# Recurrence of a hybrid HGRN2 / RWKV-7 layer: inverse levels laid over the whole array, reordered score, y and token products, loads in two parts

## The chip, the cores and the metric

One NeuronCore of a Trainium2 chip. The metric is the device time of one execution in microseconds (us). All data is fp32. [...]

## The reference

One step of a hybrid layer for 2048 tokens of a new stream ("prompt") and 8 running streams of 16 tokens ("sample"). RMSNorm and modulation; an input projection; two groups of heads on the same input; an output projection; a two-level mixture of experts; a final RMSNorm. The change is in the two groups of heads:

```
HGRN2, 4 heads of 128:     S_t = diag(f_t) S_{t-1} + k_t v_t^T,  o_t = S_t^T q_t   (chunks of 64 tokens)
RWKV-7, 8 heads of 64:     S_t = S_{t-1}(diag(w_t) - kk_t^T (a_t*kk_t)) + v_t^T k_t,  y_t = S_t r_t
```

with a normalisation and a gate on o and y, and the last states as outputs.

## The kernel before, in words

The program has four stages, each with its own block of engine programs and semaphores: `project`, `recur`, `merge`, `experts`. `project` leaves in DRAM the scaled factors of both groups (`rk`: five rows A0, A1, B0, B1, V for RWKV; `hk`: six level factors, B, KD, Q, K for HGRN2) and token rows (`tm`). Only `recur` is changed.

`recur` goes over 17 frames of 128 tokens (two chunks of 64 on the two halves of the partitions); frame 16, `TAIL`, holds the sample. In pass i of the main loop the front of frame f = i is interleaved with the back of frame b = i - 1. The order of each engine's instructions is written out by hand; semaphores tie the engines.

**Front of a frame.** `turn` transposes V, B0 and B1 into tokens (ScalarE copies them, `keep_tok`). `products` forms B·A for B0 and B1, 16 products of 64x64 by 128 columns each, and VectorE masks them (`mask_products`) into LB (the strictly causal matrix to be inverted, and its y part) and MK. RWKV's delta rule needs for every head and chunk the inverse of a 64x64 unit triangular matrix. It is built by doubling, levels 1 to 5 (in `TAIL` to 3): `begin_xt` and `turn_x0` set up level 0, and at each level `make_y` forms Y = L·X, VectorE masks it (`mask_y`), `turn_x` transposes X, ScalarE copies the transpose (`keep_xt`), `make_x` multiplies XT and Y and adds into X's bank, and ScalarE copies X (`keep_x`). The last level is `make_xt`, kept by `keep_xtf`. Each of these steps is 16 matmuls of 64x64 by 64, for 8 heads and 2 chunks; input rows `chunk(c)` always give output partitions `chunk(c)`. Beside the levels `score` forms HGRN2's seven score matrices, two a time in one bank (the last alone), VectorE merges them under level masks (`mask_score`), `turn_kd` transposes KD, and `from_tokens` starts g and y from the values.

**Back of a frame.** Chunk by chunk: `h_update`, `h_inter`, `h_intra` (HGRN2); `from_state`, `from_values`, `solve` (with the inverse), `to_state`, `y_from_state`, `y_out` (RWKV). Then VectorE and ScalarE normalise and gate o and y into `mix`, which SyncE stores.

PSUM: P_X, P_Y, P_XT, P_S serve the inverse, the products, the scores and the HGRN2 update in turn; P_ST (half used) the RWKV state, P_O o, P_EO g and y.

**Loads.** SyncE issues all. `load_front(f)` brings rk and hk of a frame with 8 DMAs on one semaphore; frame i + 2 is requested when KD of frame i is transposed (`kd_made`). `load_back` brings A, B and the token rows. At the start all loads of front 0 and the two `even` masks stand ahead of the first wait.

The sequence of TensorE around the levels, before:

```
                for lv in range(2, levels(f)):
                    make_y(f, lv)
                    turn_x(f, lv - 1)
                    score(f, lv - 1)
                    if lv < levels(f) - 1:
                        make_x(f, lv)
                    else:
                        make_xt(f)
                turn_kd(f)
                from_tokens(f)
```

Of the kernel before, what the change touches and what calls it, by code (L numbers as in the profile page):

```python
# [22 lines left out]
CH = 64  # L23
# [863 lines left out]
def recur(nc, t, bonus, ends):  # L887

    names = []
    with ExitStack() as ctx:  # L890
# [28 lines left out]
        Y = sb("Y", [128, 8, CH])  # L919
        Y1, Y3, Y5 = [sb(f"Y{n}", [128, 8, CH]) for n in (1, 3, 5)]  # L920
# [20 lines left out]
        sumd = sb("sumd", [128, 2, 4, RW_N])  # L941
# [8 lines left out]
        P_X, P_Y, P_XT, P_S, P_ST, P_O = [ctx.enter_context(nc.psum_tensor(f"re_P{b}", [128, 512], F32)) for b in range(6)]  # L950
# [3 lines left out]
        TAIL = PT  # L954

# [38 lines left out]

        block = ctx.enter_context(nc.Block())

        @block.sync
        def _(eng):
            eng.dma_start(const[:, :, :].rearrange("p a b -> p (a b)"), t["const"]).then_inc(ev("const_in"), 16)
            rk3 = t["rk"].rearrange("(c s p) w -> p c s w", p=128, s=N_RK)  # L1000
            hk3 = t["hk"].rearrange("(c s p) w -> p c s w", p=128, s=N_HK)

            def load_front(f):

                k, p = 128 * f, f % 2
                for c in range(4):
                    eng.dma_start(rkf[p][:, c, :, :], rk3[:, c, :, k:k + 128]).then_inc(ev(f"front_in{p}"), 16)
                for c in range(4):
                    if f < TAIL:
                        eng.dma_start(hkf[p][:, c, :, :], hk3[:, c, :, k:k + 128]).then_inc(ev(f"front_in{p}"), 16)  # L1010
                    else:
                        for s0, s1 in ((0, levels(f)), (N_LEVELS, N_HK)):
                            eng.dma_start(hkf[p][:, c, s0:s1, :], hk3[:, c, s0:s1, k:k + 128]).then_inc(ev(f"front_in{p}"), 16)
# [9 lines left out]
            load_front(0)  # L1023
            eng.dma_start(even[:, :, :].rearrange("p a b -> p (a b)"), t["even"]).then_inc(ev("const_in"), 16)
            eng.dma_start(even_row[:, :], t["even_row"]).then_inc(ev("const_in"), 16)
# [3 lines left out]
            load_front(1)  # L1029
            load_back(1)  # L1030
            eng.dma_start(Sd[:, :, :, :], t["state_hgrn"][0].rearrange("s h k v -> k s h v")).then_inc(ev("state_in"), 16)
# [30 lines left out]
        def _(eng):  # L1062
            eng.wait_ge(ev("const_in"), 48)


            def h_update(b):
# [4 lines left out]
                eng.wait_ge(ev("xtf_kept"), 2 * b + 2)  # L1071
                for h in range(4):
                    o = slice(128 * h, 128 * h + 128)
                    for c in range(2):
                        ins = eng.matmul((P_S, P_XT)[c][:, o], kdT[p][chunk(c), o], tmb[p][chunk(c), 0, o], start=(h == 0), stop=(h == 3), skip_group_check=True)
# [47 lines left out]
            def from_values(b, c):  # L1123

                p = b % 2
                if b or c:
                    eng.wait_ge(ev("st_kept"), 2 * b + c)
                for h in range(8):
                    eng.matmul(out_st(half(h), h), tok[p][chunk(c), 2, 64 * h:64 * h + 64], tok[p][chunk(c), 0, 64 * h:64 * h + 64],
                               start=(h < 2), stop=False, skip_group_check=True)  # L1130

            def solve(b, c):

                p = b % 2
                eng.wait_ge(ev("g_kept"), 2 * b + c + 1)
                for h in range(8):
                    ins = eng.matmul(out_g(chunk(c), h), XTF[p][chunk(c), h, :], G[chunk(c), 64 * h:64 * h + 64],
                                     start=False, stop=(h == 7), skip_group_check=True)
# [28 lines left out]

            def products(f, kind, banks):

                p = f % 2  # L1170
                for h in range(8):
                    o = 128 * (h // 2)
                    for c in range(2):
                        ins = eng.matmul(banks[h % 2][chunk(c), o:o + 128].rearrange("p (a b) -> p a b", a=2), rkf[p][half(h), h // 2, kind, chunk(c)],
                                         rkf[p][half(h), h // 2, RK_A0:RK_A1 + 1, chunk(c)], start=(h < 2), stop=(h >= 6), skip_group_check=True)
# [3 lines left out]
            def turn_x0(f):  # L1179

                eng.wait_ge(ev("xt0_made"), 2 * f + 2)
                for h in range(8):
                    for c in range(2):
                        ins = eng.matmul(P_S[chunk(c), 64 * h:64 * h + 64], XT0[chunk(c), h, :], ident[chunk(c), chunk(c)], start=(h == 0), stop=(h == 7), skip_group_check=True)
                ins.then_inc(ev("x0_made"), 1)

            def make_y(f, lv):

                if lv == 1:
                    eng.wait_ge(ev("x0_kept"), f + 1)  # L1190
                    eng.wait_ge(ev("product_kept"), 4 * f + 4)
                for g in range(2):
                    if lv > 1:
                        eng.wait_ge(ev("x_kept"), before(f, 8) + 2 * (lv - 2) + g + 1)
                    for h in range(4 * g, 4 * g + 4):
                        for c in range(2):
                            ins = eng.matmul(P_Y[chunk(c), 64 * h:64 * h + 64], LB[f % 2][chunk(c), h, 0, :], X[chunk(c), h, :],  # L1197
                                             start=(h == 0), stop=(h % 4 == 3), skip_group_check=True)
                ins.then_inc(ev("y_made"), 1)

            def turn_x(f, lv):

                for h in range(8):
                    for c in range(2):
                        ins = eng.matmul(P_XT[chunk(c), 64 * h:64 * h + 64], X[chunk(c), h, :], ident[chunk(c), chunk(c)], start=(h == 0), stop=(h == 7), skip_group_check=True)  # L1205
                ins.then_inc(ev("xt_made"), 1)

            def make_x(f, lv):

                for g in range(2):  # L1210
# [1345 lines left out]
```

## Time and profile before

| what | value |
|---|---|
| median of 3 runs | 3289.81 us (3288.94 to 3295.39) |
| the profiled execution | 3291.22 us, its span 3289.4 us |
| granted clock over the span | 0.963 |
| `project` (0 to 1105.6) | TensorE busy 1023.2 of 1105.6 us |
| `recur` (1105.6 to 1848) | TensorE busy 643.4 of 742.4 us, VectorE 403.0, ScalarE 213.3 |
| `merge` and `experts` (1848 to the end) | TensorE busy 1349.6 of 1441.4 us |

Times in the rows are us from the start of the span. In the profile PE is TensorE's matmuls, PEld its weight loads, DVE VectorE, ACT ScalarE, SPq the issuing of DMAs by SyncE. Every fp32 matmul is recorded as two, so 16 matmuls stand as x32. Matmul ends are modelled; starts are better to go by.

### The profile page before, as it was taken

The numbers are of one execution on the slowest core, as the hardware profiler recorded it, in microseconds if no ns is written. First come the engines' busy times: TensorE is split into PE (matmuls) and PEld (weight loads), VectorE is DVE, ScalarE is ACT, GpSimd is POOL, SyncE is SP. The second block draws the span as 40 slices with busy tenths as digits, with TensorE's granted clock in tenths as the row PEclk, the third lists the DMA queues.
The fourth block names the chain that finished last, engine by engine and source line by source line (L and its number), as shares of the span: only waits on it lengthen the run. The fifth ranks groups of instructions, "written<-read, shape, count | busy, mean of one in ns | idle before, by whom it ended". The sixth has DMA issues, their size and how long they took to land. (4 is left out here: it accounts for less than half of the span.)

```text
span 3289.4 us, 68115 instructions
## 1 busy us (share of the span) xinstructions
PE 3016.1 (92%) x28667; PEld 1817.9 (55%) x28668; DVE 1407.8 (43%) x3436; ACT 977.0 (30%) x1872; POOL 161.9 (5%) x248
## 2 busy tenths in 40 slices
PE   5998999999999399999998599958999999999998
PEld 2432455454545288888888355535555555555543
DVE  2255466655557355555556244452111122111217
ACT  2456334333434223332333112111222222222215
POOL 0000000000000000000000000000000000000004
PEclk8999999999999799999999699978999999999998
DMA  7631123232322755555552643355786577667658
GB/s 269 214 116 55 49 97 129 104 126 91 122 83 101 224 151 150 150 152 159 158 158 74 182 172 115 115 169 168 290 333 240 185 279 283 239 251 281 236 201 332
DMA packets 373225, 575.73 MB, mean 175 GB/s; under 512 B 31230, under 2 KB 230966, under 8 KB 369944
## 3 DMA queue, kind: packets, MB, share of 16 engines
q1 hardware_dynamic: 340296, 474.06, 42.7%
q0 software_dynamic: 18080, 72.10, 6.3%
q10 hardware_dynamic: 14640, 26.49, 2.7%
q8 instruction: 167, 2.74, 0.3%
q14 instruction: 42, 0.34, 0.0%
HBM read 427.04 MB, written 145.54 MB: 174 GB/s over the span
## 5 line engine op out<-in xcount | busy, mean ns | idle before, releaser
L451 PE MATMUL pj_P<-pj_hT,pj_wc 128*128 128x448 f32 (+2 forms) x1600 | 590.4, 516 | 0.9 <-ACT pj_stage L579 0.9
L2429 PE MATMUL moe_PG<-wgu,moe_xT 128*64 128x256 f32 x5248 | 582.1, 380 | 0.7 <-ACT moe_xT L2327 0.7
L2429 PEld LDWEIGHTS moe_PG<-wgu,moe_xT 128*64 128x64 f32 x5248 | 377.3, 137 | 226.3 <-issue 47.4
L451 PEld LDWEIGHTS pj_P<-pj_hT,pj_wc 128*128 128x128 f32 x1600 | 294.1, 189 | 256.5 <-issue 239.4
L2436 PE MATMUL moe_PTY<-wd,moe_hT 128*64 128x512 f32 x1312 | 317.7, 603 | 0.0
L2330 ACT ACT_TABLE_LOAD x82 | 105.2, 1283 | 484.2 <-issue 484.1
L1916 PE MATMUL merge_PO<-merge_w,merge_mT 128*128 128x512 f32 x544 | 244.4, 608 | 3.5 <-DMA merge_w<-in_w_out 3.5
L1916 PEld LDWEIGHTS merge_PO<-merge_w,merge_mT 128*128 128x128 f32 x544 | 104.6, 195 | 130.2 <-issue 130.2
L2289 DVE TENSOR_TENSOR moe_sg<-moe_sg,moe_PG 128x128 f32<-128x128 f32 x164 | 46.3, 282 | 283.9 <-ACT moe_sg L2330 283.9
L2293 DVE COPY moe_hT<-moe_PH 128x128 f32<-128x128 f32 x164 | 47.8, 291 | 279.9 <-PE moe_PH L2421 279.9
L2436 PEld LDWEIGHTS moe_PTY<-wd,moe_hT 128*64 128x64 f32 x1312 | 81.9, 136 | 120.2 <-issue 86.8
L2296 DVE COPY moe_y<-moe_PTY 128x512 f32<-128x512 f32 x82 | 56.7, 692 | 208.3 <-PE moe_PTY L2436 208.3
L1197 PE MATMUL re_P<-re_X,re_LB 64*64 64x64 f32 x2656 | 97.4, 220 | 28.4 <-ACT re_X L1448 23.0
L372 PE MATMUL pj_P<-pj_wt,pj_hT 128*128 128x512 f32 x272 | 122.5, 604 | 0.0
L482 PE MATMUL pj_P<-pj_wt,pj_hT 128*128 128x512 f32 x272 | 121.3, 599 | 0.0
L1197 PEld LDWEIGHTS re_P<-re_X,re_LB 64*64 64x64 f32 x2656 | 85.7, 135 | 36.4 <-ACT re_X L1448 29.7
L600 ACT ACTIVATE pj_rk<-pj_P,pj_keep_mu 128x448 f32<-128x448 f32 (+1 forms) x60 | 35.9, 602 | 196.9 <-DVEq L866 91.5
L1454 ACT COPY re_XT<-re_P 128x256 f32<-128x256 f32 x132 | 42.7, 375 | 167.6 <-PE re_P L1205 167.6
L2332 ACT ACTIVATE moe_sg<-moe_PG 128x128 f32<-128x128 f32 x82 | 22.8, 278 | 233.2 <-PE moe_PG L2429 233.2
L482 PEld LDWEIGHTS pj_P<-pj_wt,pj_hT 128*128 128x128 f32 x272 | 50.3, 190 | 67.7 <-issue 67.7
L2025 DVE TENSOR_TENSOR merge_x<-merge_PO,merge_maps 128x1024 f32<-128x1024 f32 x17 | 20.8, 1225 | 154.3 <-PE merge_PO L1916 115.4
L372 PEld LDWEIGHTS pj_P<-pj_wt,pj_hT 128*128 128x128 f32 x272 | 51.6, 195 | 59.6 <-issue 59.6
(384 smaller groups left out, 4274.2 us busy)
## 6 DMA issues: line engine op xcount, KB each, us to landing
wgu<-in_w_gate SPq DMA_DIRECT2D x32, 2048.0 KB, 9.3
wgu<-in_w_up SPq DMA_DIRECT2D x32, 2048.0 KB, 15.0
wd<-in_w_down SPq DMA_DIRECT2D x32, 2048.0 KB, 16.7
re_hkf<-scratch_hk SPq DMA_DIRECT2D x64, 640.0 KB, 8.4
re_rkf<-scratch_rk SPq DMA_DIRECT2D x68, 320.0 KB, 5.0
scratch_hk<-pj_hk SPq DMA_DIRECT2D x16, 1344.0 KB, 5.8
scratch_y_rows<-moe_y ACTq DMA_DIRECT2D x164, 128.0 KB, 5.2
scratch_rk<-pj_rk SPq DMA_DIRECT2D x16, 1120.0 KB, 4.4
```

The costliest lines, as they stand in the source:

```text
L372: ins = eng.matmul(P[2 + m % 2][:, :], hT_cols(m)[:, k, :], wt[:, k, :], start=(k == 0), stop=(k == KD - 1))
L451: ins = eng.matmul(bank[:, 0:wp], wc[:, j, k, :], hT[:, k, k0:k0 + wp], start=(k == 0), stop=(k == KD - 1), skip_group_check=True)
L482: ins = eng.matmul(PQ[:, :], rows[:, k, :], wt[:, k, :], start=(k == 0), stop=(k == KD - 1))
L1197: ins = eng.matmul(P_Y[chunk(c), 64 * h:64 * h + 64], LB[f % 2][chunk(c), h, 0, :], X[chunk(c), h, :], start=(h == 0), stop=(h % 4 == 3), ...
L1454: eng.copy(XT[:, 4 * g:4 * g + 4, :], heads(P_XT[:, 256 * g:256 * g + 256], 4)).then_inc(ev("xt_kept"), 1)
L1916: ins = eng.matmul(PO[:, half, :], mT[:, n % 2, k, :], w[:, k, 512 * half:512 * half + 512], start=(k == 0), stop=(k == KD - 1))
L2289: eng.tensor_tensor(sg[:, j, :], sg[:, j, :], gate, ALU.mult).then_inc(ev("silu_made"), 1)
L2293: eng.tensor_copy(hT[:, j, :], PH[:, j, 0:128]).then_inc(ev("hT_kept"), 1)
L2296: eng.tensor_copy(y[:, :], PY[:, :]).then_inc(ev("y_kept"), 1)
L2330: eng.activation(sg[:, 0, :], PG[:, 0, 0:128], ACT.Sigmoid).then_inc(ev("sigmoid_made"), 1)
L2429: ins = eng.matmul(PG[64 * c:64 * c + 64, j, 0:256].rearrange("p (a b) -> p a b", a=2), x_rows, wgu[p][:, :, k, o:o + 128], start=(k == 0) ...
L2436: ins = eng.matmul(PY[64 * n:64 * n + 64, :], hT[:, j, 64 * c:64 * c + 64], wd[p][:, 2 * c + j, 512 * n:512 * n + 512], start=(j == 0 and ...
```

## The change

What is changed:

- **Inverse, levels 2 and up.** Heads 0 to 3 (g = 0) keep input chunk c on output partitions of chunk c; heads 4 to 7 (g = 1) put it on the other half, in another bank. A second such step brings it back. One Y buffer per level holds the identity and takes Y by predicated copy, so `make_x` gives the new X without adding to the old. Waits are for both halves of a copy. Banks: X in P_A/P_B columns 0 to 255, XT in columns 256 to 511, Y in P_C/P_D.
- **Scores** are made one matrix a time in the free half of P_ST: `AHEAD` ones before `make_y`, `beside` ones after `turn_x`. `y_out` goes behind `make_x` of level 2, the g part of `from_tokens` in front of `make_y` of level 5.
- **One solve beside products.** The solve of chunk 0 is interleaved, head by head, with the chunk-1 half of the B0 products, and so stands behind the transposes of V, B0 and B1.
- **VectorE and ScalarE.** y's bonus, centre, variance and o's scale and gate are spread over levels 2, 3 and 4; y's root stands before the copy of XT(4); y's scale and finish behind `keep_xtf`.
- **Loads in two parts.** rk of frame i + 2 is requested once frame i's products are made, hk at `kd_made`. At the start SyncE loads only the identity and rk before the back loads; ScalarE's queue issues the other constants and hk of frame 0; the `even` masks come late.

The diff, cut to its core:

```
+        AHEAD = {2: (), 3: (1,), 4: (3,), 5: (5,)}
+        def beside(f, lv):
+            return range(2 * lv - 4, 2 * lv - 3 if lv < levels(f) - 1 else levels(f) + 1)
...
+            eng.dma_start(ident, t["const"][:, 128 * C_ID:128 * C_ID + 128]).then_inc(ev("ident_in"), 16)
...
             for i in range(TAIL + 1):
-                eng.wait_ge(ev("kd_made"), i + 1)
                 if i + 2 <= TAIL:
-                    load_front(i + 2)
+                    eng.wait_ge(ev("product_made"), 4 * i + 4)
+                    load_rk(i + 2)
+                    eng.wait_ge(ev("kd_made"), i + 1)
+                    load_hk(i + 2)
...
+            def products_and_solve(f, kind, banks, b):
+                eng.wait_ge(ev("g_kept"), 2 * b + 1)
+                for h in range(8):
+                    ins = solve_head(b, 0, h)
+                    product(f, kind, banks, h, 1)
+                ins.then_inc(ev("sa_made"), 1)
+                for h in range(8):
+                    ins = product(f, kind, banks, h, 0)
+                    if h >= 6:
+                        ins.then_inc(ev("product_made"), 1)
...
+            def make_y(f, lv):
+                eng.wait_ge(ev("x_kept"), before(f, 8) + 2 * (lv - 1))
+                for h in range(4):
+                    for g in range(2):
+                        for c in range(2):
+                            ins = eng.matmul((P_C, P_D)[g][chunk(c ^ g), 64 * h:64 * h + 64], LB[f % 2][chunk(c), 4 * g + h, 0, :], X[chunk(c), 4 * g + h, :],
+                                             start=(h == 0), stop=(h == 3), skip_group_check=True)
+                ins.then_inc(ev("y_made"), 1)
...
             def make_x(f, lv):
+                eng.wait_ge(ev("xt_kept"), before(f, 8) + 2 * (lv - 1))
+                eng.wait_ge(ev("y_kept"), before(f, 10) + 2 * lv)
+                for h in range(4):
+                    for g in range(2):
                         for c in range(2):
-                            ins = eng.matmul(P_X[chunk(c), 64 * h:64 * h + 64], left[chunk(c), h, :], right[chunk(c), h, :],
-                                             start=(lv == 1 and h == 0), stop=(h % 4 == 3), skip_group_check=True)
+                            ins = eng.matmul((P_A, P_B)[g][chunk(c ^ g), 64 * h:64 * h + 64], XT[chunk(c), 4 * g + h, :], Y[lv - 1][chunk(c), 4 * g + h, :],
+                                             start=(h == 0), stop=(h == 3), skip_group_check=True)
...
                 if f:
-                    eng.wait_ge(ev("x_kept"), before(f, 8))
-                turn(f, RK_V, P_X)
-                if f:
-                    eng.wait_ge(ev("y_kept"), before(f, 10))
-                turn(f, RK_B0, P_Y)
+                    eng.wait_ge(ev("xtf_kept"), 2 * f)
+                turn(f, RK_V, P_A)
+                turn(f, RK_B0, P_B)
                 if back:
-                    solve(b, 0)
                     eng.wait_ge(ev("s_kept"), 2 * f)
-                turn(f, RK_B1, P_XT)
+                turn(f, RK_B1, P_C)
...
-                score(f, 0)
-                if back:
-                    y_out(b)
                 for lv in range(2, levels(f)):
+                    for n in AHEAD[lv]:
+                        score(f, n)
+                    if lv == 5:
+                        from_tokens(f, 0)
                     make_y(f, lv)
                     turn_x(f, lv - 1)
-                    score(f, lv - 1)
+                    for n in beside(f, lv):
+                        score(f, n)
                     if lv < levels(f) - 1:
                         make_x(f, lv)
                     else:
                         make_xt(f)
+                    if lv == 2 and back:
+                        y_out(b)
                 turn_kd(f)
-                from_tokens(f)
+                if f == TAIL:
+                    from_tokens(f, 0)
+                from_tokens(f, 1)
...
+            eng.dma_start(const[:, 1:, :].rearrange("p a b -> p (a b)"), t["const"][:, 128:]).then_inc(ev("const_in"), 16)
+            for c in range(4):
+                eng.dma_start(hkf[0][:, c, :, :], hk3[:, c, :, 0:128]).then_inc(ev("hk_in0"), 16)
```

## Rows read from the trace of the kernel before

**Rows 1.** Windows: us, PE, PEld, DVE, ACT, POOL busy, clock, DMA share, GB/s.
```profile
1163.00:1790.00 627.00, 582.71 (x15439) 540.18 (x15436) 362.66 (x827) 195.16 (x492) 0.00 (x0) 1.00 0.53 147
```

**Rows 2.** TensorE's timeline through one frame: start, busy us, engine, line, tiles, count.
```profile
1480.16 1.16 PE L1075 MATMUL re_P<-re_tmb,re_kdT 64*128 64x128 f32 x16
...
1496.49 1.15 PE L1249 MATMUL re_P<-re_hkf 128*64 128x64 f32 x32
...
1503.49 1.15 PE L1197 MATMUL re_P<-re_X,re_LB 64*64 64x64 f32 x32 [0.47 <-ACT re_X L1448]
1504.47 1.10 PE L1205 MATMUL re_P<-re_const,re_X 64*64 64x64 f32 x32
1505.50 1.15 PE L1249 MATMUL re_P<-re_hkf 128*64 128x64 f32 x32
1506.58 1.15 PE L1217 MATMUL re_P<-re_Y,re_XT 64*64 64x64 f32 x32
1508.20 1.15 PE L1197 MATMUL re_P<-re_X,re_LB 64*64 64x64 f32 x32 [0.47 <-ACT re_X L1448]
...
1510.21 0.69 PE L1249 MATMUL re_P<-re_hkf 128*64 128x64 f32 x16
1510.85 1.15 PE L1217 MATMUL re_P<-re_Y,re_XT 64*64 64x64 f32 x32
...
1516.36 0.66 PE L1257 MATMUL re_P<-re_const,re_hkf 128*128 128x128 f32 x4
1516.95 1.15 PE L1267 MATMUL re_PEO<-re_tok,re_MK 64*64 64x64 f32 x32
...
1518.96 1.16 PE L1075 MATMUL re_P<-re_tmb,re_kdT 64*128 64x128 f32 x16
```

**Rows 3.** TensorE's timeline: `h_update` of the first and of the last full frame.
```profile
1163.72 0.49 PE L1075 MATMUL re_P<-re_tmb,re_kdT 64*128 64x128 f32 x4
...
1757.82 1.16 PE L1075 MATMUL re_P<-re_tmb,re_kdT 64*128 64x128 f32 x16
```

**Rows 4.** TensorE's timeline: solve, products; the sample's state products.
```profile
1484.36 1.14 PE L1137 MATMUL re_PEO<-re_G,re_XTF 64*64 64x64 f32 x16
...
1486.02 1.10 PE L1174 MATMUL re_P<-re_rkf 64*64 64x128 f32 x32
...
1809.92 1.91 PE L1394 MATMUL re_PEO<-re_STd,re_hkf 64*32 64x64 f32 x128
```

**Rows 5.** Timeline of the copy engines: a pair on ScalarE, one on VectorE.
```profile
1504.68 0.76 DVE L1599 TENSOR_TENSOR re_Y<-re_P,re_const 128x256 f32<-128x256 f32 x2 [1.61 <-PE re_P L1197]
...
1505.62 0.65 ACT L1454 COPY re_XT<-re_P 128x256 f32<-128x256 f32 x2 [1.91 <-PE re_P L1205]
```

**Rows 6.** VectorE's timeline: the end of y and the update of S.
```profile
1480.52 0.69 DVE L1679 TENSOR_TENSOR re_mix<-re_yc,re_tmb 128x512 f32<-128x512 f32 x1
1481.37 2.35 DVE L1563 SCALAR_TENSOR_TENSOR re_S<-re_S,ends,re_P 128x128 f32<-128x128 f32 x8 [0.16 <-PE re_P L1075]
```

**Rows 7.** Timeline at the start of the stage.
```profile
1105.97 3.69 SPq L1007 DMA_DIRECT2D re_rkf<-scratch_rk  x4
...
1120.15 0.43 SPq L1025 DMA_DIRECT2D re_even_row<-in_even_row  x1
...
1124.68 2.82 PE L1165 MATMUL re_P<-re_const,re_rkf 128*128 128x128 f32 x12 [31.35 <-DMA re_even_row<-in_even_row]
```

**Rows 8.** TensorE's timeline behind the last frame: the sample's first products.
```profile
1794.81 1.97 PE L1358 MATMUL re_P<-re_tmb,re_att 64*64 64x128 f32 x16 [4.52 <-issue]
```

**Rows 9.** Waits of TensorE (total us, times, longest), then its timeline in frame 0.
```profile
PE re_P L1205 <- issue: 3.2, 3, 1.1
...
PE re_P L1217 <- issue: 0.7, 1, 0.7
...
1155.35 0.38 PE L1197 MATMUL re_P<-re_X,re_LB 64*64 64x64 f32 x5 [2.17 <-issue]
1155.52 1.68 PE L1205 MATMUL re_P<-re_const,re_X 64*64 64x64 f32 x32
```

More of the change, by code:

```diff
@@ L1127, in from_values @@
                     eng.wait_ge(ev("st_kept"), 2 * b + c)
+                if c == 0:
+                    eng.wait_ge(ev("scored"), before(b, 7) + levels(b) + 1)
                 for h in range(8):
@@ new lines, in first_x @@
+            def first_x(f):
+                for g in range(2):
+                    eng.wait_ge(ev("y_kept"), before(f, 10) + g + 1)
+                    for h in range(4):
+                        for c in range(2):
+                            ins = eng.matmul((P_A, P_B)[g][chunk(c), 64 * h:64 * h + 64], XT0[chunk(c), 4 * g + h, :], Y[0][chunk(c), 4 * g + h, :],
+                                             start=(h == 0), stop=(h == 3), skip_group_check=True)
+                ins.then_inc(ev("x_made"), 1)
@@ L1251, in score, with from_tokens @@
                 ins.then_inc(ev("score_made"), 1)
             def turn_kd(f):
[L1255 removed]
                 for h in range(4):
[L1257 removed]
+                    ins = eng.transpose(P_C[:, 128 * h:128 * h + 128], hkf[f % 2][:, h, HK_KD, :], ident)
                 ins.then_inc(ev("kd_made"), 1)
[L1260 removed]
+            def from_tokens(f, y):
@@ L1264, in from_tokens @@
                     eng.wait_ge(ev("sa_kept"), 2 * f)
-                for h in range(8):
-                    for c in range(2):
-                        eng.matmul(out_g(chunk(c), h), MK[chunk(c), h, 0, :], tok[p][chunk(c), 0, 64 * h:64 * h + 64],
-                                   start=(h < 2), stop=False, skip_group_check=True)
-                if f:
                     eng.wait_ge(ev("y_centred"), f)
@@ L1310, in _ @@
                     from_values(b, 1)
-                make_y(f, 1)
+                first_y(f)
                 if back:
                     solve(b, 1)
-                make_x(f, 1)
+                first_x(f)
                 if back:
@@ L1480, in _ @@
                 for lv in range(2, levels(f)):
+                    if back and lv == 5:
+                        y_root(b)
                     keep_xt(f, lv - 1)
-                    if back and lv == 2:
+                    if back and lv == min(4, levels(f) - 1):
                         eng.wait_ge(ev("y_centred"), b + 1)
@@ L1601, in mask_score @@
-            def mask_score(f, r):
-                if 2 * r > levels(f):
-                    return
-                eng.wait_ge(ev("score_made"), before(f, 4) + r + 1)
-                out = att[f % 2][:, :, :]
-                for n in range(2 * r, min(2 * r + 2, levels(f) + 1)):
-                    src = heads(P_S[:, 256 * (n % 2):256 * (n % 2) + 256], 4)
-                    if n == 0:
-                        eng.tensor_tensor(out, src, eye[:, :].unsqueeze(1).to_broadcast([128, 4, CH]), ALU.mult).then_inc(ev("scored"), 1)
-                    else:
-                        eng.wait_ge(ev("scored"), before(f, 7) + n)
-                        eng.copy_predicated(out, level_mask(C_LEVEL, n - 1).bitcast(U32).unsqueeze(1).to_broadcast([128, 4, CH]), src).then_inc(ev("scored"), 1)
+                    src = P_C[:, 256 * g:256 * g + 256] if lv == 1 else (P_C, P_D)[g][:, 0:256]
@@ L1740, in _ @@
                     o_scale(TAIL)
+                    o_gate(TAIL)
             y_centre(TAIL)
```

254 lines of the change are left out of this document (130 added, 124 removed).

## The prediction

> **What bounds the kernel now.** I read the busy shares by slice first, then the engines' busy times by stage, then TensorE's timeline through one frame of the recurrence, then what ScalarE and VectorE do in the same frame, then the list of waits. The change touches only the recurrence. In its body TensorE is busy 582.7 of 627 us at the full granted clock, VectorE 362.7, ScalarE 195.2, DMA about half [rows 1]: TensorE sets the pace. A frame (128 tokens) starts with `h_update`; one clean frame runs from 1480.16 to 1518.96, 38.8 us [rows 2], and 15 frames from 1163.72 to 1757.82 average 39.6 [rows 3]; the 0.8 more are pauses named below.
>
> In the frame, `make_y`, `turn_x` and `make_x` of one level are 16 products of 64x64 each, recorded as 32 pieces (every fp32 product is two). Each takes about 1.0 us to the next start: 1503.49, 1504.47, 1505.50 [rows 2]. All 16 lie on two of the array's four 64x64 squares, because rows and output columns carry the same chunk. One level takes 4.71 us (1503.49 to 1508.20), of which TensorE waits 0.46 for the copy of X [rows 2]. So the levels are bound by the array, with a short wait for a copy.
>
> **What two more squares are worth.** `solve`, all on one square, is busy 1.14 us with 16 pieces [rows 4]; less the last one's tail of about 0.2, that is 63 ns a piece. `make_y` on two squares: 31 ns. `products` is already on four, with 128 columns a piece instead of 64: 1.10 us busy with 32 pieces [rows 4], in the same way 29 ns a piece, or 116 ns a square. So four squares do run side by side. With 64 columns a square needs 62 ns (2 x 31), over four 15.5 ns, 0.50 us for 32 pieces. From below: the sample's state products, on eight narrower tiles, run 128 pieces in 1.91 us, under 15 ns apart [rows 4], so pieces can be issued that densely. From above: nothing gained, 31 ns. I take 15.5, from `products`, nearest in shape and order.
>
> [...]
>
> **A level after the change.** Lags from the rows: the last piece ends 0.20 us after the next group could start (1.15 busy against 0.98 of spacing), an engine starts 0.05 later, a pair of half copies takes 0.65 on ScalarE and 0.76 on VectorE, TensorE goes on 0.05 later [rows 2, 5]. From the start of `make_y` = 0: `make_y` to 0.50; `turn_x` to 1.00, its last piece ends at 1.20; XT is copied 1.25 to 1.90; Y is masked 0.75 to 1.51; a score set (16 pieces and the change of shape, 0.64, from 1510.21 to 1510.85 [rows 2]) fills 1.00 to 1.64; `make_x` starts at 1.95, ends at 2.65 and issues to 2.45; X is copied 2.70 to 3.35; the next `make_y` starts at 3.40. The level is now bound by the two copies in turn: 3.40 us for 4.71. What formerly began after half a copy now waits for both halves; that is in the 3.40. The score set ahead of `make_y` (2.45 to 3.09) lies under the X copy.
>
> Splitting seven score matrices into seven sets instead of four costs 0.2 each (0.64 x 2 against 1.08 for a set of two [rows 2]), 0.6 in all; two of the three lie under the copies.
>
> Now the part from 1496.49 to the next `h_update` at 1518.96, 22.47 us today [rows 2]. Level 2: 2.45, then `y_out` 0.98 and one score 0.64: 4.07. Level 3: 3.40. Level 4: 2.45, then a score 0.64 and the token products for g 0.98: 4.07. Level 5: `make_xt` at 1.95, but VectorE has y's variance, o's scale and gate (4 operations of 0.68 to 0.69 and a small one) before it masks Y; by my account it finishes at 6.06 after level 4's start, so `make_xt` goes at 2.05; then 0.50, `turn_kd` 0.59 and the second token products 1.00 [rows 2]: 4.15. Sum 15.7: 6.8 less.
>
> **The front of the frame**, 16.33 us today (1480.16 to 1496.49). One solve beside products: 1.08 and 0.93 to the next starts today; after it the solve (8 heads of two pieces on one square, 1.0) runs beside the half of the products on two other squares, and the other half takes 0.93: 1.93, so 0.08 saved. Bounds: 0.9 saved if the second half also overlaps, 0.4 lost if the mixed shapes issue in turn. A wait comes back: VectorE ends y's last operation 1.05 us after `h_update` starts (1481.21) and then updates S in 2.35 [rows 6]. After the change its four closing operations start only when XTF is kept (15.1 in the count above) and end at about 17.9, against 15.7 for `h_update`; S is ready at 20.35, but TensorE comes to `turn` B1, which needs that bank, at 19.9. The solve that covered this is now behind it. 0.45 lost. Queued behind the waiting transpose are all of TensorE's work and ScalarE's third token copy. Front: 16.7. Frame: 32.4 for 38.8, 6.4 saved; 15 frames save **95 us**.
>
> Edits that I cost at nothing, with their cover: the wait on `xtf_kept` before the first transposes (kept 3.8 us earlier); the wait on `scored` before the state's value products (some 4 us earlier); the first score's wait for ST (kept at 0.6 after `make_y(2)`, wanted at 1.0); y's square ahead of the copy of X(4) on ScalarE (ends 0.1 before X is there: the thinnest cover, 0.6 us a frame if gone); y's root before XT(4) (1.8 us early). SyncE issues rk now after the products and hk at the frame's end. Behind hk's four DMAs stand the mix store and the back loads, wanted only a frame later. The 5.8 MB of a frame (147 GB/s [rows 1] over 39.6) took 0.53 of 39.6, 21 us [rows 1], of the 32 there are then. Cover gone would show as SP-released waits of TensorE.
>
> **Start, first and last frame.** Today TensorE starts at 1124.68, released by the DMA of `even_row`, issued at 1120.15 behind the loads of front 0 [rows 7]. After it wants only the identity and four rk DMAs, issued by about 1110 (the four take 3.7 us); with 7 us to land (even_row's took 4.5) it starts at 1117: **8 us** saved (0 to 10). The first frame takes 39.0 us [rows 3, 7] and has no back part, two pauses and a half-clock stretch: 4 to 12 saved, less up to 2 for hk, which now shares the queues: **7**. In the last frame VectorE is the limit: TensorE's next products start at 1794.81 after 4.5 us idle, held by the sample's masks, which VectorE makes behind the end of y [rows 8]. There levels 2 and 3 put three scores, y's centre, variance and o's scale and gate before XTF on VectorE; I count 1.2 later there and 0.3 for the front: **1.5 lost**.
>
> **Pauses in issue.** Between 1163 and 1790 TensorE stops 14 times, on six lines, where the profile shows no release ("issue"): 10.7 us in all, from 3.2 on the first line to 0.7 on the last [rows 9]. They come in the DMA-heavy third of a frame. In the first frame one holds the last five pieces of a `make_y` for 2.4 us, and the groups behind it run at half clock: `turn_x` takes 1.68 [rows 9] instead of 1.10. I read them as late instructions (straight-line code; no row names the cause). The code must arrive a fifth faster now, so I add half: **5 lost** (0 to 20).
>
> Sum: 95 + 8 + 7 - 1.5 - 5 = 103.5. The profiled run took 3291.2 us (span 3289.4) and the median is 3289.8, so 3187.7 for such a run and **3186** as a median.
>
> **Rivals.**
> 1. *Issue floor.* Pieces of this shape may have a floor between the 15 and 31 ns of the rows; at the middle, 23 ns, 32 take 0.75: `make_x` starts at 2.45, the next level at 4.15, the level part becomes 18.6 instead of 15.7: 2.9 x 16 = 46 back, **3232**. For: no row has four squares at 64 columns. Against: the denser pieces of the narrower tiles. [...]
> 2. *Squares don't overlap in this order* (the two output banks alternate within a chunk, in `products` between row halves). 32 pieces take 1.0, make_x starts at 3.0, a level takes 4.95, the level part 21.8; only the start and 0.3 a frame remain: **3280**. Against: `products`.
> 3. *Copies become the queue.* VectorE has 22.9 us of work a frame (362.7 of 627 [rows 1], over 39.6) in 32; if each hand-over comes 0.7 late (a score mask or y operation in front of a Y mask), 4 x 0.7 x 15 = 42 back: **3228**. For: the cover on both engines is 0.1 to 0.4 us in level 4 and 5.
> 4. *Slower: instructions arrive late.* Place: the level part, where TensorE wants 64 instructions in 0.5 us instead of 1.0, beside DMAs. Price: the first frame's pause, 2.4 us and about 2.6 at half clock over five groups, 5 in all. It decides from 21 such pauses in the stage (104/5), 1.3 a frame; at 1.5 a frame, 24 x 5 = 120: **3306**. Against: one pause of that kind today, in the first frame.
>
> **How the numbers follow.** Forecast 0.75 (its own 3168 to 3215, from 0.9 gained or 0.6 lost at the solve and ScalarE's cover, 0 to 20 of pauses); rival 1 0.07; rival 2 0.05; rival 3 0.08; rival 4 0.05. The range, 3168 to 3232, adds rival 3 and half of rival 1, and leaves out the rest and the forecast's ends. 0.2% of the time, 6.6 us, is what can be told from no change: faster 0.92 (with most of rival 2), same 0.03, slower 0.05.
>
> **What would show it.** Right: 32 pieces of `make_y` in level 3 busy about 0.70 us; level 3 to 4 3.4 us; frames 32 to 33; waits of TensorE for the copies of XT (0.3) and X (0.3) at every level; about 0.45 before the third transpose; TensorE's first product near 1117. Wrong: 0.8 or more for 32 pieces (1, 2); Y masks that start well after `make_y`'s end (3); more than 20 "issue" pauses or half clock inside the stage (4).

## The result and the profile after

The kernel after takes **3253.56 us** (median of 4 runs, 3251.47 to 3259.31) where the kernel before took 3289.38 beside it (4 runs): ratio 0.9891, 95% interval 0.9873 to 0.9909. That is 36 us saved, not 103.5, and outside the range on record.

The head of its page, and its stage windows (columns: stretch, its length, busy time and instructions of PE, PEld, DVE, ACT and POOL, granted clock as a share of full speed, DMA share, GB/s). The first window is the 15 frames, the other is explained below.

```profile
span 3249.6 us, 68199 instructions
...
PEclk8999999999999799999998799969999999999998
DMA  7631123242322685566641743455786478667658
```

```profile
1157.00:1718.00 561.00, 501.38 (x14652) 452.74 (x14648) 342.25 (x778) 180.81 (x465) 0.00 (x0) 0.96 0.59 161
...
1441.30:1444.40 3.10, 3.10 (x76) 2.98 (x74) 1.81 (x4) 1.01 (x4) 0.00 (x0) 0.50 0.01 3
```

Against [rows 1], TensorE is now busy 89% of the frames instead of 93%, and its clock is 0.96 instead of 1.00. It needs less time and stands still more. TensorE's timeline at the two ends of the 15 frames, and at the first product, answers to [rows 3, 7]:

```profile
1118.94 0.87 PE L1186 MATMUL re_P<-re_const,re_rkf 128*128 128x128 f32 x3 [27.28 <-DMA re_rkf<-scratch_rk]
...
1157.12 1.57 PE L1091 MATMUL re_P<-re_tmb,re_kdT 64*128 64x128 f32 x16
...
1717.73 1.16 PE L1091 MATMUL re_P<-re_tmb,re_kdT 64*128 64x128 f32 x16
```

The first frame's back begins 6.6 us earlier than before. 15 frames take 560.6 us for 594.1: 37.37 each for 39.61. From there to the span's end it is 1531.9 us for 1531.6; in the runs below that compute the reference this stretch takes 1529 to 1534, so 0.3 can't be told from nothing. So 6.6 + 33.5 - 0.3 = 39.8, the difference of the two spans.

Now one frame, 1419.6 to 1456.9: its TensorE timeline from the middle of the front to level 3 (start, busy us, line, shape, pieces, idle before and what ended it). It answers to [rows 2].

```profile
1433.03 1.03 PE L1230 MATMUL re_P<-re_X,re_LB 64*64 64x64 f32 x27 [0.17 <-issue]
1433.90 0.92 PE L1152 MATMUL re_PEO<-re_G,re_XTF 64*64 64x64 f32 x13
...
1434.83 1.04 PE L1240 MATMUL re_P<-re_Y,re_XT 64*64 64x64 f32 x28
...
1436.23 0.63 PE L1135 MATMUL re_PEO<-re_ST,re_arb 64*64 64x64 f32 x13
1436.66 0.56 PE L1251 MATMUL re_P<-re_X,re_LB 64*64 64x64 f32 x21
1440.07 0.39 PE L1251 MATMUL re_P<-re_X,re_LB 64*64 64x64 f32 x10 [2.84 <-issue]
...
1440.91 1.06 PE L1300 MATMUL re_P<-re_hkf 128*64 128x64 f32 x16
1441.89 1.13 PE L1271 MATMUL re_P<-re_Y,re_XT 64*64 64x64 f32 x32
1442.80 1.84 PE L1177 MATMUL re_PEO<-re_SA,re_LB 64*64 64x64 f32 x32
1444.58 0.69 PE L1300 MATMUL re_P<-re_hkf 128*64 128x64 f32 x16
1445.19 0.69 PE L1251 MATMUL re_P<-re_X,re_LB 64*64 64x64 f32 x32
1445.70 0.65 PE L1260 MATMUL re_P<-re_const,re_X 64*64 64x64 f32 x32
1446.28 0.69 PE L1300 MATMUL re_P<-re_hkf 128*64 128x64 f32 x16
1447.12 0.69 PE L1271 MATMUL re_P<-re_Y,re_XT 64*64 64x64 f32 x32
1447.74 0.69 PE L1300 MATMUL re_P<-re_hkf 128*64 128x64 f32 x16
1448.58 0.69 PE L1251 MATMUL re_P<-re_X,re_LB 64*64 64x64 f32 x32 [0.15 <-ACT re_X L1502]
```

Two things are to be seen. From 1445.19 on the level is what was predicted: 32 pieces start the next group after 0.51 us, and `make_y` to `make_y` takes 3.39 us. In front of it stands what wasn't: `make_y` of level 2 stops after 21 pieces for 2.84 us, with nothing in the profile that releases it, and then runs at half clock (the window 1441.30:1444.40, clock 0.50; 16 score pieces take 1.06 us instead of 0.69, `y_out` 1.84).

**What it stops for.** Counting pieces (the x column) from the pause at 1433.03 to the one at 1440.07, with the short rows that are left out above, gives 128, and each piece is recorded with a weight load of its own (PEld):

```profile
1433.03:1437.30 4.27, 4.20 (x128) 4.06 (x128) 1.53 (x4) 1.54 (x6) 0.00 (x0) 1.00 0.96 301
```

Counted in this way, the 48 pauses of the 15 frames have 47 distances. The first row says how many there are of a length, the second counts pieces, the third all that the trace records of TensorE between two pauses (matmuls, weight loads, and the waits and register instructions among them):

| distances | 19 | 11 | 7 | 5 | 2 | 1 | 1 | 1 |
|---|---|---|---|---|---|---|---|---|
| pieces | 127 to 128 | 252 to 256 | 379 to 383 | 506 to 509 | 634 | 761 | 889 | 1016 |
| instructions | 255 to 258 | 511 to 513 | 767 to 769 | 1022 to 1025 | 1280 | 1535 | 1792 | 2048 |

The stops fall on a grid of 256 instructions: all 47 distances lie within 2 of a multiple. The DMA view of 1437.0 to 1437.5 (rows: queue and kind, packets, MB, share) has the other half:

```profile
q1 hardware_dynamic: 319, 0.16, 115.7%
q8 instruction: 1, 0.02, 14.4%
```

Over the 15 frames, of the kernel after and of the kernel before:

```profile
q8 instruction: 116, 1.90, 1.4%
```

```profile
q8 instruction: 116, 1.90, 1.3%
```

116 packets in both, 1.90 MB or 16 KB a packet, close to 8 a frame. I take them for TensorE's code: from the first of the 48 pauses to the last the trace records 28927 instructions of TensorE and 113 packets, 256 for each (runs e10 and e11 below add instructions and get packets). Between the start of the last such packet and the end of a pause lie, in us:

| pauses | number | shortest | longest | mean |
|---|---|---|---|---|
| after, over 1 us | 18 | 2.41 | 2.80 | 2.60 |
| after, the others | 30 | 2.24 | 2.87 | 2.53 |
| before | 15 | 2.20 | 2.67 | 2.43 |

So each of the 48 pauses, and each of the 15 before the change, ends 2.2 to 2.9 us after the start of a packet; a moment taken at random in these frames lies so behind one only one time in seven (116 x 0.7 of 561 us). This is the closest that the traces come to the cause. Between 1433 and 1437 q8 brought none, at 1437.38 one, and TensorE went on at 1440.07. I read the resumption at 1433.03 as the moment from which the next block can be asked for (it lies one block earlier; no row shows the request): 4.35 us to the packet, and 2.69 from there to the first instruction. The second part is as long in short pauses (the table), so a long one arises ahead of the packet: where two pauses are one block apart, the packet starts 2.9 us after the resumption before it if the second pause is over 1 us (the mean of 8), and 1.7 if it is shorter (of 11). Meanwhile the 16 DMA engines were full of the loads of the next frames (1434.6 to 1440.6: share 1.03). In the levels of another frame, with the queues empty, packets at 1560.06 and 1564.38 were followed by resumptions at 1562.91 and 1566.67 after pauses of only 0.30; there the packet came 1.1 and 1.5 us after the resumption before it, not 4.35.

The longest of the 48 stops is 3.65 us, of the 15 before 1.42. Before the change, 128 pieces of the levels took some 4.7 to 5.2 us; now they take 3.4 to 3.9, and the next 16 KB have to come within that.

TensorE's waits over the span answer to [rows 9] (us, times, longest):

```profile
PE re_P L1251 <- issue: 9.6, 8, 2.8
PE re_P L1260 <- issue: 9.5, 11, 2.7
...
PE re_P L1300 <- issue: 7.6, 6, 3.7
PE re_PEO L1177 <- issue: 7.4, 4, 2.4
...
PE re_P L1271 <- issue: 5.8, 5, 3.2
...
PE re_P L1271 <- ACT re_XT L1508: 2.7, 18, 0.2
...
PE re_P L1251 <- ACT re_X L1502: 1.5, 6, 0.7
```

**Why the loads lie there.** SyncE's issues in the same frame (start, length of the group's issue, line):

```profile
1418.61 5.43 SPq L1024 DMA_DIRECT2D re_hkf<-scratch_hk  x4
1424.09 3.72 SPq L1059 DMA_DIRECT2D scratch_mix<-re_mix  x1
1427.85 2.42 SPq L1033 DMA_DIRECT2D re_arb<-scratch_rk  x4
...
1432.03 4.80 SPq L1017 DMA_DIRECT2D re_rkf<-scratch_rk  x4
```

rk (4 DMAs of 320 KB; hk has 4 of 640 KB) waits on SyncE's queue behind hk, the mix store and the back loads, and is issued from 12.4 us into the frame. Mean DMA share in steps of 3 us from `h_update`, worked out from windows over 9 frames (the fourth to the twelfth) of each kernel (e4, e6 and e9 are experiments, below):

| us into the frame | 12 | 15 | 18 | 21 | 24 | 27 | frame mean |
|---|---|---|---|---|---|---|---|
| before | 1.09 | 0.94 | 0.50 | 0.02 | 0.01 | 0.02 | 39.61 |
| after | 0.99 | 1.08 | 0.90 | 0.05 | 0.02 | 0.02 | 37.37 |
| e9 | 1.12 | 0.95 | 0.84 | 0.04 | 0.02 | 0.02 | 36.16 |
| e4 | 0.99 | 0.43 | 0.26 | 0.36 | 0.19 | 0.32 | 35.86 |
| e6 | 0.25 | 1.01 | 1.10 | 1.03 | 0.51 | 0.17 | 38.06 |

The dense levels begin about 17 us into the frame. In the kernel after, 30.3 of 49.1 us of pauses end between 18 and 24 us.

### The profile page after: what moved, and what is told of

It reads as the page before. It is cut to its first block and busy times, and to the rows that moved or that the text cites. A ratio compares the mean times of both kernels' runs of the same rounds, so it can differ in the third digit from the quotient of the medians.

```text
span 3249.6 us, 68199 instructions
## 1 busy us (share of the span) xinstructions
PE 2959.1 (91%) x28667; PEld 1753.5 (54%) x28668; DVE 1411.0 (43%) x3438; ACT 973.6 (30%) x1872; POOL 161.1 (5%) x248
## 5 line engine op out<-in xcount | busy, mean ns | idle before, releaser
L1300 PE MATMUL re_P<-re_hkf 128*64 128x64 f32 x1872 | 86.8, 237 | 8.6 <-issue 7.6
L482 PEld LDWEIGHTS pj_P<-pj_wt,pj_hT 128*128 128x128 f32 x272 | 50.3, 190 | 67.7 <-issue 67.7
L1655 DVE COPY_PREDICATED re_Y<-re_const,re_P 128x256 f32<-128x256 uint32 x166 | 64.6, 442 | 49.9 <-PE re_P L1230 25.4
L2439 POOL DMA_INDIRECT moe_xg<-scratch_h,moe_row x83 | 80.6, 971 | 67.1 <-POOL moe_row L2436 67.1
## 6 DMA issues: line engine op xcount, KB each, us to landing
wd<-in_w_down SPq DMA_DIRECT2D x32, 2048.0 KB, 16.6
```

Of the source, the lines that this page charges most:

```text
L482: ins = eng.matmul(PQ[:, :], rows[:, k, :], wt[:, k, :], start=(k == 0), stop=(k == KD - 1))
L1300: ins = eng.matmul(P_ST[chunk(c), 256 + 64 * h:320 + 64 * h], hkf[p][:, h, a, chunk(c)], hkf[p][:, h, b, chunk(c)], start=(h == 0), stop=( ...
L1655: eng.copy_predicated(Y[lv - 1][:, 4 * g:4 * g + 4, :], level_mask(C_LEVEL_T, lv).bitcast(U32).unsqueeze(1).to_broadcast([128, 4, CH]), he ...
L2439: eng.indirect_dma_start(xg[:, :], None, t["h2"].rearrange("t (h c) -> (t h) c", h=2), bass.IndirectOffsetOnAxis(ap=row[:, 0:1], axis=0)). ...
```

## The experiments

My theory after the two traces: late code eats the gain, and the loads of the next frames make it late. Rivals: the four squares give little by themselves; the order of work costs; the code is late even without loads. "Pauses" below are TensorE's "issue" pauses in the 15 frames, counted in its timeline, "long" ones are over 1 us. Before: 15 pauses, 10.9 us in all, 5 long with 5.8. After: 48 with 49.1, 18 long with 37.0.

**Almost no loads.** In the kernel after (e1), and in the kernel before as a control (e2), the rk, hk and back loads of frames 2 to 15 bring one partition instead of 128. These frames then work on the data of frames 0 and 1, so neither kernel computes the reference. What follows the last `h_update` then takes some 20 us longer (1554.7 and 1551.2 us, for 1531.9 and 1531.6; I take it that the router picks other experts), so that the totals are not comparable and the frames are.

```
+                    q = slice(0, 128 if f < 2 or f == TAIL else 1)
+                    eng.dma_start(rkf[p][q, c, :, :], rk3[q, c, :, k:k + 128]).then_inc(ev(f"rk_in{p}"), 16)
-                    eng.dma_start(rkf[p][:, c, :, :], rk3[:, c, :, k:k + 128]).then_inc(ev(f"rk_in{p}"), 16)
```

> The changed kernel with the frame loads of frames 2 to 15 cut to one partition of 128: as many DMAs and waits, hardly any bytes; these frames compute on the data of frames 0 and 1. Theory (late instructions): TensorE's straight-line code arrives by DMA and queues behind the frame loads; without them the long pauses (1 to 3.7 us) and the half clock behind them go, small pauses of 0.2 to 0.4 in the dense levels may stay: frames 33 to 34 us instead of 37.4, total 3185 to 3205, granted clock in the body near 1.0. Rival (the pauses come from the new order of waits, not from the queues): 37 us a frame and 3245 to 3255 as now.

> The kernel before with the same cut of its frame loads (frames 2 to 15 on one partition). Late instructions: its 14 pauses (10.7 us) go, frames 38.6 instead of 39.6: 3272 to 3280. If pauses have another cause: 3287 to 3290. Against e1 it also gives what the new order is worth when instructions are not late: 75 to 100 us.

e1: frames 33.74, 36 pauses with 16.0 us, of which 2 long (3.0); 3221.1 us. e2: frames 38.52, no pause in them; 3293.0 us. The frames came as expected; both totals are above what was expected, by about the 20 us just named. Windows over the frames of e1 and of e2:

```profile
1157.00:1680.00 523.00, 495.47 (x15000) 449.25 (x15002) 351.76 (x800) 185.96 (x474) 0.00 (x0) 1.00 0.10 31
```

```profile
1163.00:1758.00 595.00, 562.69 (x15072) 524.13 (x15072) 350.63 (x805) 189.84 (x478) 0.00 (x0) 1.00 0.08 26
```

The loads cost the kernel after 3.63 us a frame, 54 in all, and the kernel before 1.1, 16 in all. Without them four squares and the new order save 4.8 a frame, 72 us in all, for 75 to 100 expected. What remains in e1, but for the two long ones, are 0.2 to 0.7 us stops in the levels, again 127 or 128 pieces apart or a multiple of that: e1's code arrives barely too late even from nearly empty queues (DMA share 0.10). Is traffic bad for the frames in another way, too? In the kernel after, 560.6 us less 49.1 of pauses and less the 22 or so that its clock of 0.96 takes (an estimate, 0.04 of 560.6) are 32.6 a frame; e1 gives 32.6 in the same way (506.1 less 16.0 and 1.3). That leaves nothing for another cause there. In the kernel before, 16 us of loads' cost stand beside 10.9 of pauses at full clock; what the other 5 are isn't shown. One nearly undisturbed frame of e1, 1427.13 to 1459.88, is used further down:

```profile
1443.29 0.69 PE L1255 MATMUL re_P<-re_X,re_LB 64*64 64x64 f32 x32
...
1447.38 0.69 PE L1255 MATMUL re_P<-re_X,re_LB 64*64 64x64 f32 x32
...
1450.77 0.79 PE L1255 MATMUL re_P<-re_X,re_LB 64*64 64x64 f32 x30 [0.15 <-ACT re_X L1506]
...
1455.14 0.63 PE L1255 MATMUL re_P<-re_X,re_LB 64*64 64x64 f32 x29
...
1459.88 1.16 PE L1095 MATMUL re_P<-re_tmb,re_kdT 64*128 64x128 f32 x16
```

**Two squares again** (e3), with all else of the change kept (in the four products of the levels):

```
-   (P_C, P_D)[g][chunk(c ^ g), 64 * h:64 * h + 64]
+   (P_C, P_D)[g][chunk(c), 64 * h:64 * h + 64]
```

> The changed kernel with every level's products on two squares again (output chunk = input chunk for all heads), all else as changed. By my forecast's account of such a level (4.95 us) frames take 38.5 and the total is about 3280; with pauses as in the kernel before, 3275 to 3290. If the squares were worth little and the reordering most, it stays near 3255.

3293.17 us, ratio 1.0023 (1.0009 to 1.0036), frames 40.14, 26 pauses with 28.1 us. The squares bring 40 us, all of the gain and a little more. Order, solve, copies and loads together are worth nothing, or 0.2% less. But this is their worth with late code in it: both the 38.5 and the 3275 to 3290 that I expected were missed, and the pauses rose from 10.9 to 28.1 us; without them e3's frame is 38.3.

**rk spread over the levels** (e4): each of its four DMAs waits for a `make_x`.

```
             def load_rk(f, i=None):
...
+                    if i is not None:
+                        eng.wait_ge(ev("x_made"), before(i, 4) + c + 1)
...
-                    eng.wait_ge(ev("product_made"), 4 * i + 4)
-                    load_rk(i + 2)
+                    load_rk(i + 2, i)
```

> The changed kernel with the four rk loads of frame i + 2 issued one at a time at make_x of levels 1 to 4 of frame i, behind nothing else, instead of in one burst. Late instructions: the 22 us of full queues at a frame's start shrink to about 17 and the dense levels meet short bursts alone: long pauses fall by half, 3215 to 3240. Rival (order of waits): 3250 to 3256.

**3228.49 us** (3227.86 to 3231.86), ratio 0.9825 (0.9805 to 0.9844): 25 us better than the kernel after, and the fastest here that computes the reference. Three windows of one frame of the kernel after, and of e4: the front, the start of the levels, the rest.

```profile
1419.60:1434.60 15.00, 14.61 (x315) 13.19 (x313) 9.43 (x23) 4.48 (x8) 0.00 (x0) 1.00 1.08 284
1434.60:1440.60 6.00, 3.16 (x128) 3.02 (x130) 1.12 (x3) 1.54 (x5) 0.00 (x0) 1.00 1.03 298
1440.60:1452.60 12.00, 11.55 (x403) 10.47 (x396) 8.72 (x20) 4.83 (x15) 0.00 (x0) 0.86 0.03 8
```

```profile
1442.90:1457.90 15.00, 14.43 (x316) 13.07 (x314) 9.69 (x23) 4.48 (x8) 0.00 (x0) 1.00 1.06 295
1457.90:1463.90 6.00, 5.15 (x199) 4.81 (x200) 2.71 (x7) 2.48 (x9) 0.00 (x0) 1.00 0.35 118
1463.90:1475.90 12.00, 11.44 (x440) 10.17 (x436) 9.40 (x22) 4.53 (x15) 0.00 (x0) 1.00 0.30 86
```

At a DMA share of 1.03 TensorE issued 128 pieces in 6 us, exactly one block; at 0.35 it issued 199. e4 has more pauses (63, 39.2 us) but short ones: 4 long (6.8 us), and the clock over its frames is 1.00 for 0.96. That the same bytes cost 1.5 us a frame less when they stand elsewhere rules out that the volume alone decides.

**The other places.** e5: e4, and at the start the loads of the back and of hk wait until rk is in; the sample's state (3 MB) is loaded in frame 15 instead of frame 0. e6: e4, and the four DMAs of hk one after another, each when the last has landed. e7: e4, with the solve of chunk 0 back between the transposes and plain `products`.

```
e5  +            eng.wait_ge(ev("rk_in0"), 64)        (SyncE before load_back(0), ScalarE's queue before hk of frame 0)
e6  +                    if c and 2 <= f < TAIL:
e6  +                        eng.wait_ge(ev(f"hk_in{p}"), 64 * (f // 2) + 16 * c)
e7  +                    solve(b, 0)                  (before turn(f, RK_B1, P_C))
e7  +                    products(f, RK_B0, (P_D, P_A))
```

> e4 with the start's loads put in order: nothing else is issued until the rk loads of frame 0 have landed, and the sample's state (3 MB) is loaded in frame 15 instead of frame 0. If the first frame is held by the volume of DMA ahead of and beside its code: TensorE's first product at 1112 to 1114 instead of 1118.4, first frame 34 to 37 instead of 38.3, total 3215 to 3224. If the first frame's pauses are another thing: only the start moves, 3222 to 3226.

> e4 with each of the four hk loads of a frame issued when the one before has landed. Late instructions, if the depth of what is queued sets the delay: the code packet follows its request by 1 to 2.5 us instead of up to 4.3, pauses in the front of the frame go, but the DMAs stretch to most of the frame; 3215 to 3235. If it is the mere share of busy DMA time: no better than e4, 3228 to 3240.

> e4 with the solve of chunk 0 back in its old place, before the transposes of B1. My forecast's account: the new place saves 0.08 us a frame of TensorE and costs 0.45 of a wait for S; with the old place 0.3 to 0.4 a frame back, 5 us: 3221 to 3225. If the wait is hidden by other lateness: 3228 to 3232.

e6: 3266.57 us, ratio 0.9936 (0.9913 to 0.996), frames 38.06, 40 pauses (61.3 us), 21 of them long (50.1). Both values that I had expected were too low: this is 38 us more than e4. The edit lowers the share in the front, where TensorE could bear it, and carries it into the levels (1.01 to 1.10 from 15 to 24 us). So a free queue during the levels is what counts; whether a shorter queue alone would help, e6 can't say, since it moved the traffic as well. e7: 3230.35 us, no difference from e4: neither the solve beside products nor the wait for S that I had priced is worth anything that shows, and no row of TensorE's waits names S.

e5: 3233.82 us (3227.3 to 3242.6), above both of its expected ranges in the median and not told apart from e4. Its profile shows why, in the waits of TensorE in the kernel after and in e5:

```profile
PE re_P L1186 <- DMA re_rkf<-scratch_rk: 27.3, 1, 27.3
```

```profile
PE re_P L1189 <- DMA re_rkf<-scratch_rk: 21.4, 1, 21.4
...
PE re_P L1195 <- ACT re_tok L1500: 5.8, 1, 5.8
```

The order does shorten the wait by 5.9 us (rk's DMAs land 6.2 us after issue, in the median, instead of 9.9). But the second row takes as much back: ScalarE now waits for rk before it issues hk, is busy with that until 1125.19, and only then copies the tokens that TensorE needs. So the first frame takes 41.8 us, where 34 to 37 were expected. The last of the 15 frames, beside which the sample's state is now loaded, takes 41.9 for e4's 36.6, with one pause of 3.90. And in that execution `project` ended 5.6 later than in the kernel after; its last product group ran at a lower clock (0.69 for 1.00), 7.67 us for 5.33, as it also did in e3's profile. That stage was not touched, and it hides effects of this size.

**All loads at `kd_made`** (e9), as in the kernel before: this undoes "loads in two parts" alone, and only in the frames (the start stays).

```
-                    eng.wait_ge(ev("product_made"), 4 * i + 4)
+                    eng.wait_ge(ev("kd_made"), i + 1)
                     load_rk(i + 2)
-                    eng.wait_ge(ev("kd_made"), i + 1)
                     load_hk(i + 2)
```

> The kernel after, but all eight loads of frame i + 2 (rk and hk) are requested together when KD of frame i is transposed, as in the kernel before. Theory (late instructions; the burst that the next frame's loads and the back loads make decides how many levels get their code late): the burst is one piece and begins earlier than rk's did in the kernel after, so it should end a few us sooner in the frame; long pauses (over 1 us) 8 to 15 for 23, frame mean 36 to 37, median 3235 to 3245. Rival (the volume of the loads decides, not where they stand): the same as the kernel after, 3248 to 3259, with over 20 long pauses. If loading in two parts helped the kernel after: above 3259.

3233.72 us (3227.67 to 3238.61), ratio 0.9836 (0.9809 to 0.9863), frames 36.16, 50 pauses with 43.6 us, 19 long with 28.6. The time is as the theory had it, the count of long pauses is not: they get shorter (1.5 us for 2.1), not fewer. Loads in two parts cost the change 18 to 20 us (frames 18, medians 20).

**More code.** Three attempts to make late code by adding instructions that do nothing, all on e1. e8: 32 empty instructions before each `make_y`. e10: 32 semaphore increments there, 128 a frame. e11: the same 128 in the front, 64 before `h_update` and 64 behind the first `h_inter`.

```
e10 +                    for _ in range(32):
e10 +                        eng.sem_inc(ev("more_code"), 1)
```

> e1 with 32 empty instructions more before make_y at levels 2 to 5 (128 a frame, half a refill of 256). Only the frames are compared, 33.7 us in e1. Late instructions: the dense levels take their 256 instructions in the 3.7 us of a refill, so 128 more cost about 1.9 us a frame: 35.2 to 35.8. [...]

> As e1_after_small_loads (loads of one partition, inputs of frames 0 and 1; totals don't compare with the reference kernel's, frames do), with 32 semaphore increments on TensorE ahead of make_y in levels 2 to 5, 128 a frame, which nothing waits for. Theory (TensorE is fed a block of 256 instructions each 3.7 us at best, and a level of 256 instructions in 3.39 us is already faster than that): 288 instructions need 4.2 us a level, frames 3 us longer than e1's 33.7, that is 36 to 38, with pauses in the levels; half a block more fetches a frame. Rival (feeding is no limit while the DMA queues are quiet): the increments lie under the copy of X and cost no more than their own issue, under 1 us a frame, frames 33.7 to 34.7. That the builder drops them is possible: then the count of fetched blocks stays 167.

> The control for e10_sem_in_levels: the same 128 increments a frame, in the front part (around the products), where TensorE uses its instructions more slowly than the feed can bring them. Theory: they cost their own issue only, frames 33.7 to 35 and no more long pauses than in e1_after_small_loads. Rival (any 128 instructions cost the same): the same frame as e10_sem_in_levels.

None of the three decides anything about a limit in the levels. e8 has 68619 instructions like e1, so the empty ones were never in the program; it is a repeat of e1 (3223.4 us, frames 33.69). The 3.7 us a block in what was expected of e8 and e10 is an estimate from resumptions one block apart (3.66 us and more in the kernel after, 3.56 to 4.12 in e1); it is no limit, since the shortest in e9 is 3.31. In e10 and e11 the increments themselves cost 0.13 to 0.17 us each, part of it at a lower clock (0.915 and 0.919 over the span, e1 0.963): frames 55.35 and 53.16 us, 3564.5 and 3533.4 in all, far above every expected value. Only the count of packets is of use. The DMA view of e1 and of e10, whole span:

```profile
q8 instruction: 167, 2.74, 0.4%
```

```profile
q8 instruction: 175, 2.87, 0.3%
```

2112 more instructions brought 8 more packets, one for every 264; e11's 2048 more brought 8 too, one for every 256. This ties q8's packets to TensorE's instructions.

## Why the prediction was wrong, step by step

**The step that failed is "Pauses in issue"**: I costed them at 5 us more than before and bounded them at 20; they and the half clock behind them cost 54 more. The frames' part of the forecast, 594.1 - 95 + 5, is 504, 33.6 a frame (15 x 6.4 is 96; the sum on record has 95). e1, which has the change without the loads' traffic, took 33.74. That the two meet so closely is in part luck: the forecast had 15.7 us of pauses in it beside all the loads, e1 has 16.0 with hardly any. With the loads it is 37.37: 54 us of the 63.7 by which the profiled span missed. I had read the cause rightly (late instructions, straight-line code, the DMA-heavy third of a frame), and then scaled the 10.7 us of before by a factor instead of asking where the heavy third will lie when the levels start earlier in it and use their code faster. Before, the burst was at 0.50 in the slice from 18 us on; after, at 0.90.

**The sentence that let it pass** is the one on SyncE: I asked whether rk and hk arrive in time for their readers. They do (no wait of TensorE on them in a frame). What they displaced, by my reading of e1 and e4, was TensorE's own code, on a queue that my list of waits did not have.

**Rival 4** had the mechanism and the place, and the wrong sign. What was to show it, more than 20 "issue" pauses or half clock inside the stage, is there. It put the turning point at 21 pauses of 5 us. There are 18 long ones, of 2.1 us on average, and 30 short ones. Pauses and what follows them cost (37.37 - 32.67) x 15 = 70 us, where 32.67 is e1's 33.74 less its 1.07 of pauses; 49 of the 70 are pauses, and the other 21 fit the 22 or so that the clock of 0.96 takes. Before it was 16 (39.61 against e2's 38.52). From 38.52 to 32.67 the change saves 5.85 a frame, 88 us; 54 of them go to the late code, not more than all.

**Squares and levels.** 32 pieces on four squares: 0.50 predicted, 0.51 measured. Level 3: 3.40 and 3.39. In e1's frame level 2 takes 4.09 (4.07), level 4 4.37 (4.07), level 5 4.74 with about half a microsecond of pause (4.15). The sum is 16.6 for 15.7. The front is 16.16 for 16.7: neither the wait for S nor the 0.08 of the solve is there (e7). 32.75 in all, for 32.4. Rivals 1 and 2 fall with the 0.51, 16 ns a piece: a floor between 15 and 31 ns would show as 0.75. Rival 3 falls too: the waits for copies are 2.7 and 1.5 us in the whole run.

**Start and first frame.** Predicted 8 and 7 saved, measured 6.6 for both. The first product starts at 1118.94 for [rows 7] 1124.68: 5.7, of which 1.7 is that `project` happened to end earlier. I let 7 us pass from rk's issue to the first product; with hk and the back loads beside it, it took 10.7 (1108.28 to 1118.94). The first frame takes 38.2 us, where it took 39.0: it stops five times, for 7.2 us, where it stopped twice for 3.4; the last stop, of 1.85 us, lies just before 1157.12, and `h_update` behind it takes 1.57 us instead of 1.16. e3, with the same loads at the start and only two squares, has two stops of 2.2 us in all there, a clock of 0.96 for 0.85, and takes 34.8. That hk and the code share the queues here too is my reading; no run takes hk away at the start alone.

**Last frame.** 1.5 lost predicted, 0.3 measured, which is within what that stretch varies.

Sum of the misses: 56.5 in the frames, 8.4 at the start, -1.2 at the end, 63.7.

## What to carry to other kernels

This straight-line program has one more input stream, TensorE's code: 16 KB for 256 instructions, 116 times in 15 frames before and after. The denser the matmuls, the less time a block leaves for the next (128 pieces of the levels last 3.4 to 3.9 us, where they lasted 4.7 to 5.2). In another kernel, count pieces between "issue" pauses, and if they come at one fixed spacing, look for the instruction queue in the DMA view. When a change makes a stretch denser, ask what the DMA queues carry in that stretch, not only whether the loads reach their readers. Then place the loads where TensorE issues slowly, or spread them so thinly that the queues are not full in the dense stretch (e4: share 0.19 to 0.43 from 15 us into the frame on); here moving four DMAs gave 25 us more to a change that had given 36. Look at the DMA share of that stretch afterwards: e6 spread its loads too, filled the levels with them (1.01 to 1.10 from 15 to 24 us) and lost 38 us.

## What the runs showed that I had not expected

- A block of code: packet to resumption 2.2 to 2.9 us, under full and empty queues alike (2.69 at 1440.07, DMA share 1.03; 2.85 and 2.29 at 1562.91 and 1566.67, share 0.02). From empty queues the pauses are 0.3 when the levels use 128 pieces in 3.4 to 3.9 us; under a full queue it was about 7 us from one resumption to the next (1433.03 to 1440.07).
- A pause of 2.84 us was followed by a stretch at clock 0.50 (1441.30 to 1444.40); in the kernel before, one of 2.17 in the first frame by another (1157.20 to 1160.00). e4's short pauses leave the clock over its frames at 1.00.
- Semaphore increments on TensorE cost 0.13 to 0.17 us each (e10: four stops of 4.1 us a frame, 32 increments each).
- `project`, the same in all kernels, ends 5 to 6 us later in some executions, with 16 large products at 7.67 us instead of 5.33. One profile does not carry a difference of that size.
- Left open: the request itself is in no row, so that reading the 4.35 us up to the packet as the time of a request is mine; and how long a frame would be with the code always there. Removing instructions from the levels was not tried.
